# Routing stage of a two-layer mixture-of-experts trunk: the shift added to the turned rows by TensorE, shorter comparisons, and a later gate on the weight loads

## The reference, cut to what matters

```python
def moe(h, w_router, b_router, w_gate, w_up, w_down):
    t = h.reshape(B * T, Dm)
    scores = jax.nn.sigmoid(jnp.einsum('nd,de->ne', t, w_router))
    sel = (scores + b_router).reshape(-1, N_EXPERT_GROUPS, EXPERTS_PER_GROUP)
    group_score = jnp.sum(lax.top_k(sel, TOP_K)[0], axis=-1)
    best = jnp.argmax(group_score, axis=-1)
    ...
    hg = jnp.einsum('nd,edf->nef', t, w_gate)
    hu = jnp.einsum('nd,edf->nef', t, w_up)
    a = jax.nn.silu(hg) * hu * gate[..., None]
    y = jnp.einsum('nef,efd->nd', a, w_down)
# in each layer, D_MODEL = 1024, D_EXPERT = 512:
h = rms_norm(y, g_ffn[l]) * (1 + sc2) + sh2
y = y + gt2 * moe(h, w_router, b_router, w_gate[l], w_up[l], w_down[l])
```

## Time and profile before

| | |
|---|---|
| time, median of 3 runs | 1133.17 us (1132.31 to 1133.34) |
| the profiled execution | 1131.33 us, span 1129.5 us, mean granted clock 0.978 |
| busy: PE, DVE, ACT, POOL | 1062.4, 850.6, 693.4, 181.8 us |
| routing stage, layer 0 | about 251 to 287.5 us of the span |
| routing stage, layer 1 | about 786 to 818.5 us of the span |

### The profile page before, as it was taken

One profiled execution on the slowest core, in us unless ns is written; L12 is line 12 of the kernel. 1 busy time (PEld: TensorE's weight loads), 2 busy tenths in 40 slices (PEclk: granted clock), 3 DMA queues, 4 the chain that ended last, 5 costly groups with the idle time before them and its releaser, 6 DMA issues.

```text
span 1129.5 us, 16096 instructions
## 1 busy us (share of the span) xinstructions
PE 1062.4 (94%) x5963; PEld 844.3 (75%) x5965; DVE 850.6 (75%) x1177; ACT 693.4 (61%) x885; POOL 181.8 (16%) x202
## 2 busy tenths in 40 slices
PE   7999998896999999999999999899699999999997
PEld 4798454683788888888868985568388888888876
DVE  5345656767999888888865546865899988888896
ACT  2323555652687777777724256755367777777764
POOL 0335200343111111110040011000301111111002
PEclk8999999997999999999999999999799999999998
DMA  9997888256999999999599463004799999999951
GB/s 353 345 345 220 321 300 282 71 171 258 354 370 365 368 376 375 373 374 386 212 389 280 149 188 128 1 1 152 299 362 375 367 370 384 375 375 369 367 195 58
DMA packets 83201, 321.99 MB, mean 285 GB/s; under 512 B 22560, under 2 KB 27054, under 8 KB 70332
## 3 DMA queue, kind: packets, MB, share of 16 engines
q1 hardware_dynamic: 67232, 285.58, 68.6%
q0 software_dynamic: 14800, 32.30, 8.5%
q10 hardware_dynamic: 1100, 3.23, 0.7%
HBM read 310.15 MB, written 30.59 MB: 302 GB/s over the span
## 4 chain that ended last, share of the span: by engine, by line
PE 84%; DVE 7%; ACT 4%; DMA 2%; issue 2%; SPq 1%; POOL 0%; DVEq 0%; ACTq 0%; POOLq 0%
PE bank L1266 16%; PE bank L1258 16%; PE bank L1259 16%; PE bank L1133 3%; PE bank L960 3%; PE bank L956 3%; PE bank L930 3%; PE bank L953 3%; PE bank L1319 2%; PE bank L1147 2%; DMA ring<-in_w_in 2%; PE bank L1025 2%; PE bank L1165 2%; PE bank L990 1%; PE bank L1066 1%
## 5 line engine op out<-in xcount | busy, mean ns | idle before, releaser
L1744 ACT ACTIVATE work_r<-ring 128x4096 fp32r<-128x4096 f32 x93 | 338.1, 3635 | 121.4 <-PE bank L1259 109.9
L2340 DVE TENSOR_TENSOR ring_r<-ring,work_r 128x4096 fp32r<-128x4096 f32 x92 | 404.2, 4417 | 2.8 <-ACT work_r L1744 2.8
L1258 PE MATMUL bank<-work_r 128*128 128x512 f32 x768 | 305.2, 397 | 4.7 <-issue 3.2
L1259 PE MATMUL bank<-work_r 128*128 128x512 f32 x768 | 300.1, 391 | 0.0
L1266 PE MATMUL bank<-ring_r,work_r 128*128 128x512 f32 x768 | 193.8, 394 | 0.0
L1258 PEld LDWEIGHTS bank<-work_r 128*128 128x128 f32 x768 | 144.8, 188 | 35.2 <-issue 4.0
L1266 PEld LDWEIGHTS bank<-ring_r,work_r 128*128 128x128 f32 x768 | 143.7, 188 | 32.4
L1259 PEld LDWEIGHTS bank<-work_r 128*128 128x128 f32 x768 | 144.4, 188 | 28.8
L2626 POOL DMA_INDIRECT work<-hscr,idx x32 | 39.9, 1247 | 280.9 <-PE bank L1319 253.5
L1587 ACT ACTIVATE work_r<-ring 128x512 fp32r<-128x512 f32 (+1 forms) x48 | 28.8, 603 | 71.4 <-PE bank L960 71.3
L2024 DVE TENSOR_TENSOR ring_r<-ring,work_r 128x512 fp32r<-128x512 f32 (+1 forms) x48 | 32.1, 676 | 50.7 <-ACT work_r L1587 50.6
(11 more groups left out here) (282 smaller groups left out, 1582.9 us busy)
## 6 DMA issues: line engine op xcount, KB each, us to landing
ring<-in_w_gate SPq DMA_DIRECT2D x32, 2048.0 KB, 10.1
ring<-in_w_up SPq DMA_DIRECT2D x32, 2048.0 KB, 10.2
ring<-in_w_down SPq DMA_DIRECT2D x32, 2048.0 KB, 10.4
ring<-in_w_ada SPq DMA_DIRECT2D x24, 2048.0 KB, 9.6
ring<-in_w_in SPq DMA_DIRECT2D x4, 2048.0 KB, 16.6
yscr<-hT POOLq DMA_DIRECT2D x2, 3072.0 KB, 12.8
ring<-yscr SPq DMA_DIRECT2D x6, 1024.0 KB, 7.2
ring<-in_w_out SPq DMA_DIRECT2D x4, 1280.0 KB, 6.5
```

What stands on the lines that cost most here:

```text
L1258: mm(b[:], x_hi[:, k, :], hi[:, k, half, :], start=(k == 0), stop=False)
L1259: last = mm(b[:], x_lo[:, k, :], hi[:, k, half, :], start=False, stop=False)
L1744: A_(w_hi[:, slot % 2, :], ring[slot][:], ACT.Copy).then_inc(s_hi, 1)
L2340: tt(ring_r[slot][:], ring[slot][:], w_hi[:, slot % 2, :].bitcast(F32), ALU.subtract).then_inc(s_lo, 1)
```

## The change

The shift's logits: POOL folds swr (shift times router weights) over its eight pieces in three halving adds, so that one matmul (into bW) replaces the eight of "shiftw". The shift of the rows: DVE makes inv = mean square times 1/rms (that is, rms); PE spreads it to rows (bI), ACT copies it (inv_rows), and PE adds, by one matmul with a single contraction row for each hr bank, rms times shift onto the turned rows; POOL's adds are gone, ACT's scaled copy gives the finished row, and the three stores go after all six copies. beaten() becomes four steps with the compare in the last. first_expert_high goes in quarters (0, 1, 2 inside the output projection, 3 behind the stores); first_expert_low does quarter 0 there and quarters 1 to 3 in one piece behind tokens_rest(0). onehots(3) moves from before tokens_rest(0) to behind it, by_slot(3) from the gate to the up product. In layer 0, B010 and A18 move ahead of the rank, B18 between by_slot(0) and by_slot(1). In both layers only down0 and later loads wait for the gather.

```diff
-    return ["A010"], ["A011"], ["B010", "B011"], ["A18", "A19", "B18", "B19"]
+    return ["A010"], ["A011", "B010", "A18"], ["B011"], ["B18", "A19", "B19"]
...
-        n += ["router", "shiftw", "routerT"] + [f"hr{t}{h}" for t in range(NT) for h in range(2)]
+        n += ["router", "routerT"] + [f"hr{t}{h}" for h in range(2) for t in range(NT)]
...
-                            if p == 0 and isinstance(i, int) and (e, kind) == (1, 2 if l else 1):
+                            if p == 0 and isinstance(i, int) and (e, kind) == (1, 2):
...
                 raw_logits(range(KT - 1))
+                pe.wait_ge(s_swr, 6 * (l + 1))
+                mm(bW, ones, swr[:, 0, :], start=True, stop=True)
                 sums_of_added(l)
...
-                pe.wait_ge(s_swr, 3 * (l + 1))
-                b = fill_begin((l, "shiftw"))
-                for k in range(KT):
-                    last = mm(b[:, 0:NT * NE], ones, swr[:, k, :], start=(k == 0), stop=(k == KT - 1))
...
+                def shift_added(h):
+                    for t in range(NT):
+                        r = slice(32 * t, 32 * t + 1)
+                        last = mm(bank((l, f"hr{t}{h}"))[:], inv_rows[r, :], shift_rows[1 if t == 0 else 0][r, 512 * h:512 * h + 512],
+                                  start=False, stop=True, skip_group_check=True)
+                        filled((l, f"hr{t}{h}"), last)
+                rows_turned_half(0)
+                pe.wait_ge(s_inv, 3 * l + 1)
+                for t in range(NT):
+                    last = mm(bI[32 * t:32 * t + 32, 0:P], inv[:, t:t + 1].to_broadcast([P, 32]), ident, start=True, stop=True,
+                              skip_group_check=True)
+                last.then_inc(s_inv, 1)
+                rows_turned_half(1)
+                pe.wait_ge(s_shin, 32 * (l + 1))
+                pe.wait_ge(s_inv, 3 * l + 3)
+                shift_added(0)
+                shift_added(1)
                 for j in route[0] + route[1]:
                     ada(j)
...
                     def slots_in_gate():
                         by_slot(2)
+
+                    def slots_in_up():
                         by_slot(3)
-
-                    def slots_in_up():
                         by_slot(4)
                         weights_by_slot()
...
                 copy((l, "router"), rlog, T)
+                act.wait_ge(s_inv, 3 * l + 2)
+                A_(inv_rows[0:96, :], bI[0:96, 0:P], ACT.Copy).then_inc(s_inv, 1)
+                act.wait_ge(s_rexp, 2 * l + 1)
+                A_(rw[:, 0, :], rw[:, 0, :], ACT.Exp, scale=-1.0).then_inc(s_rexp, 1)
...
+                for h in range(2):
+                    for t in range(NT):
+                        copy((l, f"hr{t}{h}"), hrow[t][:, 512 * h:512 * h + 512], 512, scale=ns[:, 1, t:t + 1])
+                for t in range(NT):
+                    read_out(act, (l, f"hr{t}1"))
                     act.dma_start(hscr[t * P:(t + 1) * P, :], hrow[t]).then_inc(s_hscr, 16)
+                first_expert_high(l, 3)
...
-                    chain(tt(c1, spread4(x, "i"), spread4(x, "j"), ALU.is_equal))
+                    chain(tt(c1, spread4(x, "i"), spread4(x, "j"), ALU.is_ge))
                     chain(tt(c1, c1, before.unsqueeze(1).to_broadcast([P, n, EPG, EPG]), ALU.mult))
-                    chain(tt(c2, spread4(x, "i"), spread4(x, "j"), ALU.is_gt))
-                    chain(tt(c1, c1, c2, ALU.add))
-                    chain(nc.vector.tensor_reduce(g4(dst), c1, AX.X, ALU.add))
+                    chain(tt(c2, c1, c1.rearrange("p g j i -> p g i j"), ALU.subtract))
+                    chain(nc.vector.tensor_reduce(g4(dst), c2, AX.X, ALU.add))
+                    place_no = cv("iota")[:, 0:EPG].unsqueeze(1).to_broadcast([P, n, EPG])
+                    chain(stt(g4(dst), g4(dst), EPG - most, place_no, ALU.add, ALU.is_lt))
...
-                    for q in range(2, NPS if p else NPS - 1):
+                    for q in range(2, NPS if p else NPS - 2):
                         onehots(q)
...
-                    if p == 0:
-                        first_expert_low(0)
                     tokens_rest(0)
                     if p == 0:
-                        first_expert_low(1).then_inc(s_lo, 1)
+                        first_expert_low(1, 4).then_inc(s_lo, 1)
+                        onehots(NPS - 2)
                         onehots(NPS - 1)
                     rest(0, 1, 1)
...
+                for i, k in enumerate((KT // 2, KT // 4, KT // 8)):
+                    g.wait_ge(s_swr, 6 * l + NT + i)
+                    nc.gpsimd.tensor_tensor(swr[:, 0:k, :], swr[:, 0:k, :], swr[:, k:2 * k, :], ALU.add).then_inc(s_swr, 1)
...
-                    nc.gpsimd.tensor_tensor(hrow[t], hrow[t], shift_rows[1 if t == 0 else 0], ALU.add).then_inc(s_hrow, 1)
```

More of the change, by code:

```diff
@@ L427, in build @@
         rlog = carve(T, 3 * D + 512)
+        inv = carve(NT)
+        inv_rows = carve(P)
         rw = c3(carve(12 * 48, 6 * D + DE), 12)
@@ L1219, in _, with rows_turned_half @@
                 filled((l, "routerT"), last)
-                for i in range(2 * NT):
-                    t, h = divmod(i, 2)
+                def rows_turned_half(h):
                     pe.wait_ge(s_zgain, KT * l + 4 * h + 4)
-                    turn4((l, f"hr{t}{h}"), lambda k: hT[:, 4 * h + k, t * P:(t + 1) * P])
+                    for t in range(NT):
+                        b = fill_begin((l, f"hr{t}{h}"))
+                        for k in range(4):
+                            mm(b[:, k * P:(k + 1) * P], hT[:, 4 * h + k, t * P:(t + 1) * P], ident, is_transpose=True,
+                               start=(k == 0), stop=False, skip_group_check=True)
+                def shift_added(h):
[15 more added lines that the diff above has]
+                shift_added(1)
                 for j in route[0] + route[1]:
@@ L1302, in experts @@
                     by_slot(0)
+                    if p == 0:
+                        for j in route[3][0:1]:
+                            ada(j)
                     by_slot(1)
                     if p == 0:
-                        for j in route[3]:
+                        for j in route[3][1:]:
                             ada(j)
@@ L1509, in out_high, with first_expert_high @@
                     A_(out_hi[half], w[:, 4 * half:4 * half + 4, (n % 4) * P:(n % 4) * P + P], ACT.Copy).then_inc(s_outw_hi, 1)
-            def first_expert_high(l, half):
+            def first_expert_high(l, quarter):
                 act.wait_ge(*moe_land(l, 0, 0, 0))
-                x = slice(CW // 2 * half, CW // 2 * half + CW // 2)
-                return A_(w_hi[:, 0, x], ring[0][:, x], ACT.Copy)
+                x = slice(CW // 4 * quarter, CW // 4 * quarter + CW // 4)
+                A_(w_hi[:, 0, x], ring[0][:, x], ACT.Copy).then_inc(s_feh, 1)
             def squares_behind_out(l):
@@ L1523, in squares_behind_out @@
                         out_high(l, n + 1)
+                    if n == KT - 2:
+                        first_expert_high(l, 0)
+                        first_expert_high(l, 1)
+                    if n == KT - 1:
+                        first_expert_high(l, 2)
                     read_out(act, (l, f"op{n}"))
@@ L1535, in squares_behind_out @@
                         copy((l, "shift"), shifts[0:2 * KT, :], P, rows=slice(0, 2 * KT))
-                    if n == KT - 2:
-                        first_expert_high(l, 0)
             def modulate(l, which):
@@ L1703, in _ @@
                 copy((l, "router"), rlog, T)
+                act.wait_ge(s_inv, 3 * l + 2)
+                A_(inv_rows[0:96, :], bI[0:96, 0:P], ACT.Copy).then_inc(s_inv, 1)
+                act.wait_ge(s_rexp, 2 * l + 1)
+                A_(rw[:, 0, :], rw[:, 0, :], ACT.Exp, scale=-1.0).then_inc(s_rexp, 1)
                 act.wait_ge(s_shout, 16 * (l + 1))
[L1707 to L1729 removed]
+                act.wait_ge(s_root, roots_before(l, 1) + 1)
+                for h in range(2):
+                    for t in range(NT):
+                        copy((l, f"hr{t}{h}"), hrow[t][:, 512 * h:512 * h + 512], 512, scale=ns[:, 1, t:t + 1])
+                for t in range(NT):
+                    read_out(act, (l, f"hr{t}1"))
+                    act.dma_start(hscr[t * P:(t + 1) * P, :], hrow[t]).then_inc(s_hscr, 16)
+                first_expert_high(l, 3)
+                act.wait_ge(s_feh, 4 * (l + 1))
+                act.sem_inc(s_hi, 1)
+                for j in (j for step in route for j in step):
                     ada_row(l, j)
@@ L2160, in out_low, with first_expert_low @@
                     tt(w_low[:, x, c], w[:, x, c], out_hi[half].bitcast(F32), ALU.subtract).then_inc(s_outw_lo, 1)
-                def first_expert_low(half):
-                    v.wait_ge(s_hi, chunk_no(l, 0, 0, 0) + 1)
-                    x = slice(CW // 2 * half, CW // 2 * half + CW // 2)
+                def first_expert_low(first, end):
+                    v.wait_ge(s_feh, 4 * l + end)
```

(13 more changed lines are left out.)

47 lines of the change are left out of this document (13 added, 34 removed).

## The result

The changed kernel takes 1139.73 us (median of 11 executions, 1135.08 to 1141.85), the kernel before 1133.31 in the same rounds (1130.64 to 1134.01): 1.0053 times, 95% interval 1.0039 to 1.0067, 6.4 us slower. The prediction had 1136.1 and a range that ended at 1139.0. The profiled execution took 1139.73 us with a span of 1137.9 and a mean granted clock of 0.973.

A forecast was written before the change was run, and what follows sets the result against it. PE, holding 84% of the chain, was taken to set the pace, with stores waiting for bandwidth. Layer 0 +2.3 and layer 1 +0.6 gave +2.9 us, 1133.17 to 1136.1; range 1129.6 to 1139.0.

The forecast's parts named there:

- 2.2 were taken: Ahead of A010 in layer 0: six single-row shift matmuls, three beside each other, take 2.2 us.
- the first rival: Shift matmuls run one after the other, 4 us more before A010 in layer 0; +2 on top, 1138; chance 0.15.
- 280.1: Layer 0: the last store lands at 280.1 instead of 273.2, because it passes beside gate1 and up1.
- 284.1: Layer 0: tokens are there at 284.1 instead of a turn at 283.79, a term of +0.3 us.
- The faster rival: Stores get about half the bandwidth beside loads, layer 0's last store lands before about 277; -3.3 us, about 1129.8; chance 0.2.
- PE stands still for most of 2.9 us in the middle of the up product: Both layers, before the slot weights: DVE's longer piece (+1.1) and onehots(3) (+1.85) make PE wait, +2.9 us each.
- +2.3: Layer 0's sum: +0.3 for the tokens, -0.9 for DVE's earlier piece, +2.9 for PE's wait.
- +0.6: Layer 1's sum: -1.9 to -2.3 for the earlier tokens' turn, +2.9 for PE's wait, less a little slack.
- the -0.9: Layer 0: DVE reaches its first_expert_low piece 3.3 us after the token turn began instead of 4.2, winning 0.9 us.
- the quarters in the projection: first_expert_high's quarters hide in ACT's waits in the projection; if that fails, about 1 us comes onto the last piece.
- one byte in five: Layer 0: a store beside a load gets about one byte in five, so nearly all 4.2 MB of loads pass first.

The follow-up runs named there:

- the experiment with up1 early: The kernel before with up1 of layer 0 no longer waiting for the gather; measured 0.9990 times the kernel before.
- the fillers: The changed kernel with ten filler products on PE just ahead of its wait for the slot weights; measured 1.0032 times the kernel before.
- its DVE order alone: The kernel before with the fourth part's one-hots made behind the tokens' low part and by_slot(3) in the up product; measured 1.0064 times the kernel before.
- weights() early: The changed kernel with DVE's weights() moved ahead of the tokens' low part; measured 0.9982 times the kernel before, 1130.37 us.
- ... and up1 waits: The changed kernel with weights() ahead of the tokens' low part and layer 0's up1 waiting for the gather again; measured 0.9946 times the kernel before.
- up1 waits: The changed kernel with up1 and later loads of layer 0 waiting for the first gather again; measured 1.0039 times the kernel before.
- ... and gate1 waits: The changed kernel with weights() ahead of the tokens' low part, gate1 and later loads waiting for the gather in both layers; 0.9913 times the kernel before, 1123.27 us.
- gate1 waits: The changed kernel with gate1 and all later loads waiting for the gather in both layers, weights() unmoved; measured 1.0003 times the kernel before.
- the fourth part's one-hots early: The changed kernel with DVE making the fourth part's one-hots ahead of the tokens' low part again; measured 1.0027 times the kernel before.

## Why the prediction was wrong

**What held.** The steps of 0.4 us and the mask 6.5 us earlier. Six shift matmuls in about 2.0 us where 2.2 were taken; three run beside each other, so the first rival falls. gate1 at 263.49 and up1 at 265.20. The last store at 280.5 where 280.1 was worked out, the gather released by it, the tokens' turn at 284.24 where 284.1 was summed; the experiment with up1 early shows that same step alone. In layer 1 the gather kept its distance to the sums of squares, 20.47 us against 21.23. The faster rival decided at a landing before 277; it came at 280.5.

**The step that failed** is "PE stands still for most of 2.9 us in the middle of the up product", and within it the price, not the wait. Layer 0 was summed at +2.3 up to the slot weights and has -0.21 + 2.30 = +2.1; layer 1 at +0.6 and has -2.78 + 2.57 = -0.2. These are 1.9 us together where 2.9 were forecast; PE stood still for 2.08 and 1.41 us of the two steps. (Of the terms of layer 0, the -0.9 came as -0.36: behind PE's wait of 5.12 us the granted clock was 0.50 from 284 to 286, the tokens' turn took 1.95 us instead of 1.05, and DVE reached its piece 3.82 us after its start.) But a wait was priced at its own length, and the next products at the length that they had in the rows of before. In its place the runs show that behind this wait the granted clock drops to 1.2 GHz, and that until it is back PE loses 2.63 us in layer 0 and 1.58 in layer 1 (the steps of the table behind the slot weights; the fillers show 2.6 for layer 0 with the wait kept). So the way from the tokens to the first activations, forecast at +2.0 in layer 0 (2.9 less 0.9) and +2.9 in layer 1, measures 2.30 + 2.63 = 4.9 and 2.57 + 1.58 = 4.2. A row that warned of it stood among those read: a clock of 0.69 over the routing of layer 0, where PE waits.

Four pairs of kernels differ in one edit of DVE's order, which decides whether PE waits there:

| kernel without the wait | with it | waits, us | ratio apart | us | rows, us |
|---|---|---|---|---|---|
| before | its DVE order alone | 1.47 + 1.48 | 0.0064 | 7.2 | 6.7 |
| weights() early | changed | 2.08 + 1.41 | 0.0071 | 8.0 | 8.3 |
| ... and up1 waits | up1 waits | 2.53 + 1.82 | 0.0093 | 10.5 | 8.2 |
| ... and gate1 waits | gate1 waits | 2.55 + 2.50 | 0.0090 | 10.2 | 8.3 |

The column "us" is the difference of the ratios by 1131 us; "rows" is how much longer the way from the tokens' turn to the turn of the first activations is in the profiles, both layers together. A microsecond of waiting cost about two: 2.0 to 2.4 by the times, 1.6 to 2.4 by the rows.

The version with the fourth part's one-hots early is a fifth such pair with the changed kernel, and it fits by the rows only. Its three profiles are 6.0 to 6.8 us shorter on that way, but its median is only 2.9 us lower. So the price of the wait is shown where it arises; where that version loses the other 3 to 4 us is open.

**What else was missed.** 1.17 us between the layers: PE waits there about 2.4 us in both kernels, but in the profiled execution of the changed one the clock fell behind it and in the kernel before it did not (below). 0.66 us ahead of the routing lies within the spread of that point over all profiles (251.3 to 255.3), so the quarters in the projection are not shown to cost anything. The two together, with 0.44 at the end, are 2.3 of the 8.4.

**The share of a store beside loads.** The prediction took one byte in five from the landing times. The queues' rows of the changed kernel fit it: 4.19 MB of loads in 288 packets are 14.6 KB each, 1.57 MB of stores in 432 packets 3.6 KB each. One packet of each in turn gives the stores 3.6 of 18.2 KB, one byte in five. In narrower windows, 129 packets of the stores and one of the loads pass from 263 to 266 us, before gate1's data move, 47 and 95 from 266 to 270, and 183 and 174 from 270 to 278, which are 0.68 and 2.59 MB. So some 300 packets of the stores were left beside as many of the loads, and both end nearly together, at 280.5 and 280.1. The Trainium skill, DMA: Bandwidth & Descriptors, section Queues, rings and completion order, has each DMA engine take turns between queues by packets. With the profile's packets taken for these, the trace agrees from 270 to 278 us, and not from 266 to 270. With gate1 held back, 7.7 us from the last store's issue were enough for a gather that did not wait for the stores any more.

## What to carry to other kernels

Before work is moved behind the point at which an engine's input arrives, look in the timeline for the next instruction that waits for the whole list, and price PE's standing still there at about twice its length: the wait, and the products that follow at half clock. Small pieces that nothing holds up belong into the idle time ahead of the late input (here 7 us of DVE), but only where that idle time exists, as the kernel before shows. And an earlier result is worth nothing while a bulk load passes in front of the transfer that carries it: with the load held back and weights() early, the same change is 10 us faster than the kernel before instead of 6 slower.

## What was not expected of the hardware

The clock after a short wait is not a matter of the wait's length alone. At the slot weights it fell behind all ten waits of 1.00 to 2.55 us, stayed at 1.00 behind one of 0.57 that followed fillers, and fell once behind 0.13. At the first product of layer 0's first expert the kernel before waits 1.38 us, and the clock stays at 1.00 from 287 to 291. At the end of layer 0's experts the same wait of PE, for nothing that the profile shows, stands in all sixteen profiles, 2.38 to 3.48 us long. In nine the mean clock of the 4 us behind it was 0.57 to 0.65, in seven 1.00, and the lengths do not sort them: 3.07 kept the clock, 2.43 lost it in the changed kernel and kept it in another. The kernel before and the changed one:

```profile
571.96 0.47 PE L1258 MATMUL bank<-work_r 128*128 128x512 f32 x1 [2.38 <-issue]
572.26 0.40 PE L1259 MATMUL bank<-work_r 128*128 128x512 f32 x1
```

```profile
577.38 0.47 PE L1282 MATMUL bank<-work_r 128*128 128x512 f32 x1 [2.43 <-issue]
...
577.94 0.63 PE L1282 MATMUL bank<-work_r 128*128 128x512 f32 x1
```

The way from the turn of layer 0's first activations to the sums of squares of layer 1 takes 482.0 to 482.2 us in five of the nine and 480.7 to 480.9 in six of the seven, so such a fall costs about 1.3 us. In one of the nine, where the clock stayed up for the first microsecond, it takes 481.0; the other four profiles have a wait above 3 us. Whether such falls make up part of the up to 8 us by which executions of one kernel differ is not shown, and what decides them was not tried.
